# Recurrent gates of a two-block model: border products on stacked activations, the four groups spread between chunks, tangents in place of sigmoids

## What is computed

```python
h = rmsnorm(x, norm_g)
u = h @ w_in                                  # 1024 x 3072
xb, gate = u[..., :1536], u[..., 1536:]
xb = causal_depthwise_conv(xb, conv_w, conv_b)      # 4 taps
xs = xb.reshape(bsz, seq, 16, 96)                   # 16 blocks of 96
r = sigmoid(einsum('bshi,hij->bshj', xs, wr) + br)  # block-diagonal
i = sigmoid(einsum('bshi,hij->bshj', xs, wi) + bi)
log_a = -8.0 * r * softplus(-lam)
a = exp(log_a)
b = sqrt(-expm1(2.0 * log_a)) * (i * xb)
hs = scan of h[t] = a[t] * h[t-1] + b[t]
x + (hs * silu(gate)) @ w_out
```

## Time and profile before

| what | value |
|---|---|
| median of three runs | 792.99 us (792.81 to 792.99) |
| the profiled execution, its own time | 792.79 us |
| its span in the trace | 791.0 us |
| granted TensorE clock, mean | 0.999 of full |
| PE, DVE, ACT, POOL busy | 782.8, 581.2, 489.5, 83.5 us |

### The profile page before, as it was taken

How to read it: one execution, slowest core, us unless ns; L and a number is a source line. 1 busy time by engine, 2 the same in 40 slices (tenths; PEclk the granted TensorE clock), 3 DMA queues, 4 the chain that set the end, 5 groups by cost and what they waited for, 6 DMA issues and landing times.

```text
span 791.0 us, 14668 instructions
## 1 busy us (share of the span) xinstructions
PE 782.8 (99%) x5381; PEld 717.9 (91%) x5381; DVE 581.2 (73%) x884; ACT 489.5 (62%) x763; POOL 83.5 (11%) x150
## 2 busy tenths in 40 slices
PE   8999999999999999999999999999999999999997
PEld 7999999998998888888888899999999888888885
DVE  5986897978967877786449665696578787787443
ACT  7779956878765655554346475764756655555434
POOL 9405100058100000000000021000000000000000
PEclk9999999999999999999999999999999999999999
DMA  8724566533546666665665554346555666665651
GB/s 271 224 80 125 170 194 207 177 119 109 175 143 186 199 193 193 190 185 202 191 187 165 181 161 152 116 140 181 164 167 171 182 206 203 187 186 184 189 184 53
DMA packets 101045, 136.30 MB, mean 172 GB/s; under 512 B 5065, under 2 KB 86401, under 8 KB 100993
## 3 DMA queue, kind: packets, MB, share of 16 engines
q1 hardware_dynamic: 99232, 133.23, 55.8%
q0 software_dynamic: 1600, 2.28, 1.1%
q10 hardware_dynamic: 160, 0.07, 0.0%
HBM read 134.51 MB, written 1.05 MB: 171 GB/s over the span
## 4 chain that ended last, share of the span: by engine, by line
PE 95%; DVE 2%; ACT 2%; DMA 1%; issue 0%; SPq 0%; ACTq 0%
PE bank L557 35%; PE bank L620 20%; PE bank L622 11%; PE bank L565 8%; PE bank L666 8%; PE bank L713 5%; PE bank L714 3%; PE bank L884 1%; PE bank L866 1%; PE bank L891 1%; DVE w_lo L1665 1%; ACT acts L1157 1%; DMA arena<-x 1%; PE bank L894 0%; ACT w_hi L1157 0%; DVE acts L1703 0%
## 5 line engine op out<-in xcount | busy, mean ns | idle before, releaser
L1665 DVE TENSOR_TENSOR w_lo<-stage,w_hi 128x1024 fp32r<-128x1024 f32 x249 | 304.0, 1225 | 133.9 <-ACT w_hi L1157 133.2
L1157 ACT ACTIVATE w_hi<-stage 128x1024 fp32r<-128x1024 f32 (+1 forms) x251 | 262.5, 1050 | 118.3 <-PE bank L557 41.1
L557 PE MATMUL bank<-acts,w_hi 128*128 128x256 f32 x1584 | 288.7, 284 | 0.4 <-DVE acts L1766 0.2
L557 PEld LDWEIGHTS bank<-acts,w_hi 128*128 128x128 f32 x1584 | 246.5, 192 | 2.6 <-issue 1.7
L620 PE MATMUL bank<-acts,w_hi 128*128 128x512 f32 x704 | 245.2, 392 | 0.0
L557 PE MATMUL bank<-acts,w_lo 128*128 128x256 f32 x792 | 224.0, 283 | 0.0
L622 PE MATMUL bank<-acts,w_lo 128*128 128x256 f32 x704 | 197.2, 280 | 0.0
L620 PEld LDWEIGHTS bank<-acts,w_hi 128*128 128x128 f32 x704 | 131.7, 187 | 29.1
L557 PEld LDWEIGHTS bank<-acts,w_lo 128*128 128x128 f32 x792 | 151.8, 192 | 0.0
L622 PEld LDWEIGHTS bank<-acts,w_lo 128*128 128x128 f32 x704 | 133.1, 189 | 0.0
L1157 ACT ACTIVATE arena<-bank 128x512 f32<-128x512 f32 (+1 forms) x79 | 43.6, 561 | 64.6 <-PE bank L622 47.7
(11 more groups left out here) (201 smaller groups left out, 764.5 us busy)
## 6 DMA issues: line engine op xcount, KB each, us to landing
stage<-ffn_w_gate SPq DMA_DIRECT2D x44, 512.0 KB, 4.5
stage<-ffn_w_up SPq DMA_DIRECT2D x44, 512.0 KB, 4.6
stage<-ffn_w_down SPq DMA_DIRECT2D x44, 512.0 KB, 3.8
stage<-w_in SPq DMA_DIRECT2D x40, 512.0 KB, 3.7
stage<-a_w_in SPq DMA_DIRECT2D x24, 512.0 KB, 4.7
stage<-b_w_in SPq DMA_DIRECT2D x16, 512.0 KB, 3.8
stage<-a_w_out SPq DMA_DIRECT2D x12, 512.0 KB, 3.6
stage<-b_w_out SPq DMA_DIRECT2D x8, 512.0 KB, 3.6
```

The source lines that it names most:

```text
L557: mm = pe.matmul(dst, w[:, slot, c:c + P], a[:, k, :] if isinstance(k, int) else a[:, bass.ds(k, 1), :], start=start and n == 0, stop=stop ...
L1157: return nc.scalar.activation(out_, in_, func, **kw)
L1665: dve.tensor_tensor(w_lo[:, n % RING, 0:w], src, w_hi[:, n % RING, 0:w].bitcast(F32), ALU.subtract)\
```

## The change

The high and the low part of the activations that a border tile needs are copied one above the other into one 128-partition tile (`stacked`, made by `stack(g)` on POOL: eight copies for a group, each waiting for the one before), and the weights of the border are laid twice (`GATE_AGAIN`, 16 more transfers of POOL). One matmul with the high weights then gives two of the three products, and one with the low weights the third and the low by low product besides. A group is 3 diagonal tiles x 3 matmuls and 3 stacked tiles x 2 matmuls, for r and i: 30 matmuls. `GATE_COLS` falls from 896 to 768.

The groups are spread: group 0 behind chunk 3, group 1 behind chunk 4, groups 2 and 3 behind the first and the second chunk of `C_G` (`H_RI` 8, 12, 18, 22). The loop on ACT and DVE now runs 24 halves. `decay(0)`, `decay(1)` and `decay(2)` stand inside it on ACT, at n = 14, 16 and 20. The product of i and xb moves from POOL to DVE (`lru_gated`).

Sigmoid(z) is written (1 + tanh(z/2))/2: the two biases are halved, the factor of the decay is halved and given as a bias too, and the root takes a factor 0.25. ACT then needs two table loads fewer. `gate_hi` moves to the tiles of `GATE`, `x_tok` to tiles 48 on, and `lam_ratio` and `lam_series` start six halves sooner.

```diff
-GATE_COLS = 896
-GATE_TILES = [(0, 0, 0), (1, 0, 256), (0, 1, 128), (1, 1, 384), (2, 1, 640), (1, 2, 512), (2, 2, 768)]
-GATE_PIECES = [(0, 0, 96, 0, 0), (1, 0, 32, 96, 96), (1, 32, 64, 0, 256 + 96),
-               (2, 0, 64, 64, 256 + 192), (2, 64, 32, 0, 640 + 64), (3, 0, 96, 32, 640 + 160)]
+GATE_COLS = 768
+GATE_MAIN, GATE_REST = [0, 512, 256], [384, 128, 640]
+GATE_PIECES = [(0, 0, 96, 0, 0), (1, 0, 32, 96, 96), (1, 32, 64, 0, 384 + 96),
+               (2, 0, 64, 64, 512 + 64), (2, 64, 32, 0, 128 + 64), (3, 0, 96, 32, 256 + 32)]
+GATE_AGAIN = [(1, 32, 64, 64, 384 + 96, 0, 32), (1, 0, 32, 64, 128, 32, 64),
+              (2, 64, 32, 32, 128 + 64, 0, 64), (2, 0, 64, 0, 640, 64, 32)]
+STACK = [(1, 0, 32, 0, 2, 0), (1, 96, 32, 0, 0, 96), (1, 32, 32, 1, 2, 0), (1, 64, 32, 1, 0, 96),
+         (0, 0, 64, 0, 1, 0), (0, 64, 64, 1, 1, 0), (2, 64, 64, 0, 1, 64), (2, 0, 64, 1, 1, 64)]
 C_X, C_G, C_AO, C_KV, C_Q, C_BG, C_BO, C_F1, C_D1 = 0, 6, 12, 18, 19, 23, 27, 31, 53
 C_MIX, C_BR, C_WO, C_F2, C_D2, C_END = 64, 84, 88, 92, 114, 125
-H_RI = [8, 14, 16, 18]
+H_RI = [8, 12, 18, 22]
...
-    return (4, 5, 7)[c % 3]
+    return (4, 5, 0, 4, 5, 7)[c]
...
+            def stack(g):
+                pool.wait_ge(xbl, (3 * g + 2) // 2 + 1)
+                for i, (m, p, n, part, k, at) in enumerate(STACK):
+                    if g or i:
+                        pool.wait_ge(stack_done, len(STACK) * g + i)
+                    pool.tensor_copy(stacked(g, m)[p:p + n, :], acts[at:at + n, 8 + 3 * g + k, part, :].bitcast(F32))\
+                        .then_inc(stack_done, 1)
...
+                if pair == 1:
+                    stack(0)
+                for w, name in enumerate(("a_gate_r_w", "a_gate_i_w")):
+                    blocks = I[name][0].rearrange("(g b) i j -> b i g j", b=4)
+                    for b, r, n, p, c, j0, jn in GATE_AGAIN:
+                        pool.dma_start(place[p:p + n, :, w, c:c + jn],
+                                       blocks[b, r:r + n, 2 * pair:2 * pair + 2, j0:j0 + jn]).then_inc(gate_in[pair], 16)
+            stack(1)
...
-            pool.wait_ge(xbl, 6)
-            for g in range(LG):
-                pool.wait_ge(ri_sig, 2 * g + 2)
-                pool.tensor_tensor(tiles(II + 3 * g, 3), tiles(II + 3 * g, 3), tiles(XB + 3 * g, 3), ALU.mult)\
-                    .then_inc(lru_bx, 1)
+            stack(2)
+            stack(3)
+            pool.wait_ge(stack_done, len(STACK) * LG)
...
                 for w in range(2):
                     half = H_RI[g] + w
                     pe.wait_ge(w_done, half + 1)
-                    if w == 0:
-                        pe.wait_ge(xbl, (3 * g + 2) // 2 + 1)
-                        if g == 1:
-                            pe.wait_ge(par_ready, 2)
-                        if g >= 2:
-                            pe.wait_ge(ri_sig, 2 * (g - 1))
-                    done = [0, 0, 0]
-                    for k, m, c in GATE_TILES:
-                        q = 3 * w + m
-                        done[m] += 1
-                        mm = passes(bank[banks[q // 2]][:, (q % 2) * T:(q % 2 + 1) * T], half % RING, c, 8 + 3 * g + k,
-                                    done[m] == 1 and q % 2 == 0, done[m] == (2, 3, 2)[m])
+                    for m, c in enumerate(GATE_MAIN):
+                        dst, first = place(w, m)
+                        passes(dst, half % RING, c, 8 + 3 * g + m, first, False)
+                pe.wait_ge(stack_done, len(STACK) * (g + 1))
+                for w in range(2):
+                    half = H_RI[g] + w
+                    for m, c in enumerate(GATE_REST):
+                        dst, _ = place(w, m)
+                        pe.matmul(dst, w_hi[:, half % RING, c:c + P], stacked(g, m), start=False, stop=False,
+                                  skip_group_check=True)
+                        mm = pe.matmul(dst, w_lo[:, half % RING, c:c + P], stacked(g, m), start=False, stop=True,
+                                       skip_group_check=True)
                     mm.then_inc(ring_free, 1)
             for c in range(6):
@@ -783,22 +819,26 @@
                         .then_inc(par_t, 1)
                 if c == 3:
                     pe.wait_ge(x_ready, 4)
-                    gates(0)
-            for g in range(1, LG):
-                gates(g)
-            pe.wait_ge(conv_x, LT)
+                if c in (3, 4):
+                    gates(c - 3)
+            pe.wait_ge(conv_x, 10)
             for c in range(6):
-                if c == 2:
+                if c == 1:
+                    pe.wait_ge(conv_x, LT)
+                if c == 3:
                     pe.wait_ge(ri_sig, 2 * LG)
-                if c >= 3:
+                if c in (3, 4):
                     pe.wait_ge(gate_raw, c - 2)
                 col_chunk(C_G + c, gate_bank(c))
-                if c == 2:
+                if c < 2:
+                    gates(2 + c)
+                if c == 3:
                     pe.wait_ge(rows_b_in, 16 * 11)
                     pe.transpose(bank[6][:, 0:ROWS_B], rows_b[:, :], con[0:ROWS_B, IDENT:IDENT + ROWS_B])\
                         .then_inc(par_t, 1)
+            pe.wait_ge(gate_raw, 3)
...
+            def decay(g):
+                act.wait_ge(ri_sig, 2 * g + 1)
+                for m in range(3):
+                    t = 3 * g + m
+                    s = f(tiles(AA + t), tiles(RR + t), ACT.Exp, scale=lam[:, 7, t:t + 1],
+                          bias=lam[:, 7, t:t + 1])
+                s.then_inc(lru_a, 1)
+                for m in range(3):
+                    t = 3 * g + m
+                    s = f(tiles(RR + t), tiles(RR + t), ACT.Tanh, scale=lam[:, 7, t:t + 1],
+                          bias=lam[:, 7, t:t + 1])
+                s.then_inc(lru_t, 1)
+            for n in range(half_of(C_G + 2)):
                 if n - 1 in x_end:
                     xb_hi(x_end[n - 1])
-                if n == 7:
+                if n == 14:
+                    act.wait_ge(lam_ready, 1)
+                if n in (14, 16, 20):
+                    decay((14, 16, 20).index(n))
+                if n == 2:
                     f(lam[:, 0, :], par_a[:, LAM:LAM + LT], ACT.Abs).then_inc(lam_e, 1)
...
-                        y = f(tiles((RR, II)[w] + t), b[:, (q % 2) * T:(q % 2 + 1) * T], ACT.Sigmoid,
+                        y = f(tiles((RR, II)[w] + t), b[:, (q % 2) * T:(q % 2 + 1) * T], ACT.Tanh, scale=0.5,
                               bias=par_a[:, (BR, BI)[w] + t:(BR, BI)[w] + t + 1])
...
-                f(tiles(RR + 3 * g, 3), tiles(RR + 3 * g, 3), ACT.Sqrt, scale=-1.0).then_inc(lru_s, 1)
-            act.wait_ge(lam_ready, 1)
-            for g in range(LG):
-                decay(g)
-                hi(24 + g)
+                f(tiles(RR + 3 * g, 3), tiles(RR + 3 * g, 3), ACT.Sqrt, scale=-0.25).then_inc(lru_s, 1)
+            decay(3)
+            hi(28)
             act.preload_act_table(ACT.Sqrt)
             lru_root(0)
-            hi(28)
             lru_root(1)
...
+            def lru_gated(g):
+                dve.wait_ge(ri_sig, 2 * g + 2)
+                i3 = tiles(II + 3 * g, 3)
+                dve.scalar_tensor_tensor(i3, i3, 1.0, tiles(XB + 3 * g, 3), ALU.add, ALU.mult).then_inc(lru_bx, 1)
+            def lru_square(g):
+                dve.wait_ge(lru_t, g + 1)
+                dve.wait_ge(lru_aa, g + 1)
+                r = tiles(RR + 3 * g, 3)
+                dve.scalar_tensor_tensor(r, tiles(XB + 3 * g, 3), 1.0, r, ALU.add, ALU.mult).then_inc(lru_m, 1)
+            def gate_out(c):
+                dve.wait_ge(ring_free, half_of(C_G + c) + 2)
+                dve.tensor_copy(tiles(GATE + 2 * c, 2), bank[gate_bank(c)][:, :]).then_inc(gate_raw, 1)
+            for n in range(half_of(C_G + 2)):
                 if n - 1 in x_end:
                     xb_lo(x_end[n - 1])
+                if n in (half_of(C_G) + 2, half_of(C_G + 1) + 2):
+                    gate_out((n - half_of(C_G)) // 4)
...
+                if n == 19:
+                    lru_gated(0)
+                if n == 20:
+                    lru_gated(1)
+                if n == 21:
+                    lru_square(0)
+                if n == 22:
+                    lru_square(1)
+                if n == 23:
+                    lru_gated(2)
...
-            lo(24)
-            gate_out(0)
-            lru_square(0)
-            lo(25)
-            lru_square(1)
-            lo(26)
-            gate_out(1)
+            lru_gated(3)
             lru_square(2)
-            lo(27)
             gate_out(2)
+            lo(28)
             lru_square(3)
-            lo(28)
             lru_input(0)
```

55 lines of the change are left out of this document (24 added, 31 removed).

## The result

The changed kernel takes 794.09 us (median of 20 executions), the kernel before 792.86 in the same measurement: a ratio of 1.0016, 95% interval 1.001 to 1.0022. The forecast was 792.0, a little faster; it came out 1.2 us slower. The profiled execution of the changed kernel took 794.71 us, with a span of 792.9.

What follows compares the result with a forecast made beforehand. The prediction took the stage as bound by TensorE's number of matmuls until ACT or DVE is late. From 792.79, - 5.78 for matmuls + 4.8 for lateness gave 791.8, and 0.2 for the median 792.0; range 789.0 to 795.0.

Steps and rivals of the forecast that it cites:

- Removed, 5.78: TensorE in the recurrent layer: 12 matmuls fewer in each of four groups, 48 x 0.1204 = 5.78 us won.
- TensorE's table: TensorE's timetable if nothing is late: half 20 needed at 63.33, half 28 at 84.29, `C_AO` starting at 95.9.
- First lateness: Half 20, behind ACT's list with two decays: ready at 65.5, needed at 63.33, so TensorE stands still 2.2 us.
- Second lateness: Half 28, behind ACT's and DVE's lists: ready at 88.5, needed at 84.29; 4.2 us late in all.
- the rival beside it: One stall only: the lateness at half 28 fails to appear, 5.78 less 2.2, time 789.4; chance 0.2.
- the 2.2 and 2.7: DVE before half 28: 2.2 us for `lru_square(0)` with POOL's square, 2.7 for POOL's squares ahead of `lru_square(2)`.
- 0.6 at half 29: Behind half 28, DVE's work through half 29 takes 3.5 us where TensorE takes 2.89: 0.6 more.
- The sum: Against the profiled 792.79: - 5.78 + 4.8 = - 1.0, so 791.8; the median of runs 0.2 higher, 792.0.
- POOL's copies: Copies for the stacked tiles: 0.45 us each, 3.6 a group; group 1's end near 48.3, no term of their own.
- the sign named for it: POOL's copies in the profile: the forecast is wrong if they last other than 0.3 to 0.6 us.
- slower, by POOL's copies: Rival: each copy costs more than 0.45; at 0.9, 3.4 us more, 795.4. Chance 0.25, of which 0.18 beyond the bound.
- y_lo: Last link, group 0, ahead of `C_AO`: ready about 98.1, needed at 100.7, so it costs nothing.

Runs made afterwards that it cites:

- the best order: Changed kernel with decays later on ACT, DVE's products in its idle time, group 1's POOL copies earlier, and the tail's splits reordered: 788.66 us, ratio 0.9948.
- the run whose clock did not fall: Changed kernel plus 17 unread matmuls ahead of half 20 and 17 ahead of half 28, to keep TensorE busy in both waits: 793.99 us.

## Why the prediction was wrong, by its own steps

- **Removed, 5.78.** Right. The pace of the pieces is unchanged, and the best order gives back 4.1 of it.
- **TensorE's table.** Right to 0.09. In the last order, where nothing waits ahead of it, half 20 starts at 63.33, and the table with the later start has 63.42.
- **First lateness: the step that failed is "a decay 2.41 (71.68 to 74.09)".** The decay before the change read only its scale from memory, the diff gives it a bias besides, and I took the old row's price for the new form. A row of before could have told: a copy of a chunk, with scale and bias, has a pace of 0.91 / 2 = 0.455, an activation out of a bank, with a bias only, 2.15 / 6 = 0.358. It measures 2.96. Two decays lie ahead of half 20, 1.1 us. The taps of chunk 4 ended at 49.33 instead of the 49.0 that I took, 0.33, of which 0.09 is the later start and 0.24 a lateness against the table. Together 1.34 of the 1.47 by which 3.67 exceeds 2.2; the other 0.13 is the way from the end of the low part (about 66.95) to TensorE's first matmul (67.09), which the sum left out. The run without the bias took the 1.1 away again (1.03). The difference is 111 ns in the mean of one activation, and (2.96 - 2.41) / 6 = 92 ns in the pace. The Trainium skill (ScalarE: Activation LUTs, "What ACT_TABLE_LOAD costs") says that each per-partition pointer operand of an activation adds about 93 ns; the pace agrees (92), the mean is somewhat above it (111), and I had not applied it.
- **Second lateness.** Right in all its places: the stretched `lru_square(0)`, the wait for POOL ahead of `lru_square(2)`, the operations in between. Its size was off by the same term: three decays, 1.65, and the 0.24 of the taps, together 1.89, where 6.11 - 4.2 = 1.91 is missing. One slip is in the rival beside it: without the lock the 2.2 and 2.7 would shrink by 3 x 1.33, not 2 x 1.33 (the 1.33 is once in the 2.2 and twice in the 2.7). Its 789.4 stays, since either removes the 2.0 in question.
- **0.6 at half 29.** Right, and visible only where the clock does not fall (0.44, 0.39 and 0.38 of printed idle time in three runs, with 0.16 each).
- **The sum**, with the decay at 2.96 and the taps at 49.33: -5.78 + 4.8 + 1.65 + 0.33 = +1.0. Measured: +1.2 in the median, +1.2 in the run whose clock did not fall. The term that was missing for TensorE's clock is worth nothing to 0.7 an execution and does not carry the sign. The mechanism was right; one price of 0.55 too little, counted three times, is enough to turn the forecast from -1.0 to +0.65, and the taps bring it to +1.0.
- **POOL's copies.** Group 1's ended at 47.9, forecast 48.3, and cost nothing, as forecast; the run with them early shows it. The price was right too: a copy that nothing stretches takes 0.41 and the next starts 0.46 after it, forecast 0.45, and with the 3 us of DVE's low parts that the forecast added group 1 was to last from 41 to 48.3 and lasted 7.30. What was wrong is the sign named for it, a copy of 0.3 to 0.6: the mean in a group holds DVE's share and came to 0.53 to 0.91. The rival "slower, by POOL's copies" gave the right sign by the wrong cause: it took 0.9 for a copy with DVE's share on top, and 0.9 was measured with that share inside.
- **y_lo.** Right in that TensorE did not wait for it. It came at 100.1 where 98.1 was forecast, later by as much as half 28.
- **The range** of 789.0 to 795.0 held the time. The chance of 0.18 for slower by more than 0.2% stood on POOL's copies alone; within 0.2%, where the ratio of 1.0016 lies, had 0.43. The bound was set too wide: the measurement tells 0.16% from no change (interval 1.001 to 1.0022). The direction that the forecast took, a small gain, is what the runs refute.

## What to carry to other kernels

Where an edit gives an activation one more operand from memory, its price need not be that of the row before (2.41 became 2.96 here), even if shape and function are the same: look for another row with as many operands from memory. Work that is taken from a bound engine is won only as far as the two engines behind it keep its new table; put their movable operations where they idle, and what the next half needs in front of what only the end needs. Here the order of the same instructions was worth 5.4 us, nearly as much as the matmuls themselves.
